# A feed-forward up projection on one Trainium2 core: high and low activations as one product of 512 columns, added by VectorE

## The reference, cut to what matters

```python
def conv_ffn(h, w_up, conv_w, conv_b, w_down):
    a, b = jnp.split(h @ w_up, 2, axis=-1)          # h: 256 x 1024, w_up: 1024 x 5632
    a = causal_depthwise_conv(a, conv_w, width=3) + conv_b
    return (jax.nn.gelu(a) * b) @ w_down            # w_down: 2816 x 1024
```

## Time and profile before

| | |
|---|---|
| Median of 3 runs | 938.27 us (937.1 to 939.4) |
| Profiled execution, its own time | 937.77 us |
| Its span, first to last instruction | 935.9 us |
| Mean granted TensorE clock over the span | 0.979 of full speed |
| Up projection, first product to last | 262.03 to 388.72 us |
| Down projection, first product | 389.73 us |
| The copies of `w_small` and `cmp_w2` | issued at 4.03 and 4.53 us, landed 10.8 and 10.6 us later |
| ScalarE's first use of `w_small` | 15.73 us |

### The profile page before, as it was taken

The page is one execution under the profiler, slowest core; times in us unless marked ns, Lnnn a source line. Parts: engine busy times, 40 slices in busy tenths (PEclk is TensorE's granted clock), DMA queues, the critical chain, the costliest instruction groups (busy, mean ns, idle before and its releaser), DMA issues.

```text
span 935.9 us, 15607 instructions
## 1 busy us (share of the span) xinstructions
PE 884.7 (95%) x6286; PEld 798.9 (85%) x6286; DVE 529.2 (57%) x931; ACT 485.3 (52%) x817; POOL 33.7 (4%) x39
## 2 busy tenths in 40 slices
PE   6999999998999999999899999999899799988987
PEld 6999898888999999987799999888777799975665
DVE  5334356758556666757745333577646736465334
ACT  6643557753465444555643344566655654443334
POOL 0000000007000000000000000000000000000310
PEclk9999999999999999999899999999999899999799
DMA  9655732245525555565354235333337355252031
GB/s 344 252 176 215 275 128 99 91 142 183 173 97 183 182 183 184 174 220 181 98 192 162 91 136 181 135 96 130 106 120 239 129 180 169 102 180 91 0 113 46
DMA packets 21555, 144.54 MB, mean 154 GB/s; under 512 B 2513, under 2 KB 3153, under 8 KB 4720
## 3 DMA queue, kind: packets, MB, share of 16 engines
q1 hardware_dynamic: 20592, 140.55, 43.4%
q10 hardware_dynamic: 896, 3.03, 1.0%
HBM read 142.53 MB, written 1.05 MB: 153 GB/s over the span
## 4 chain that ended last, share of the span: by engine, by line
PE 79%; DVE 9%; ACT 7%; issue 3%; DMA 2%; POOL 0%; DVEq 0%; POOLq 0%; ACTq 0%; SPq 0%
PE PS L417 77%; DVE wl L1582 3%; ACT wh L1088 2%; DMA ring<-w 1%; ACT PB L1122 1%; PE PS L492 1%; ACT L1447 1%; ACT hh L1102 1%; DMA xa<-x 1%; PE PS L1018 0%; ACT L1451 0%; PE PS L688 0%; DVE PB L1985 0%; DVE hl L1602 0%; DVE Y L2009 0%
## 5 line engine op out<-in xcount | busy, mean ns | idle before, releaser
L1582 DVE TENSOR_TENSOR wl<-ring,wh 128x1024 fp32r<-128x1024 f32 x248 | 305.0, 1233 | 312.7 <-ACT wh L1088 305.3
L1088 ACT ACTIVATE wh<-ring 128x1024 fp32r<-128x1024 f32 x248 | 261.2, 1056 | 292.2 <-PE PS L417 273.9
L417 PE MATMUL PS<-hh,wh 128*128 128x256 f32 x1244 | 357.9, 288 | 6.6 <-DVE BIG L2117 3.7
L417 PE MATMUL PS<-hl,wh 128*128 128x256 f32 x1244 | 352.1, 283 | 0.0
L417 PE MATMUL PS<-hh,wl 128*128 128x256 f32 x1244 | 351.9, 283 | 0.0
L417 PEld LDWEIGHTS PS<-hh,wh 128*128 128x128 f32 x1244 | 238.7, 192 | 12.4 <-issue 5.8
L417 PEld LDWEIGHTS PS<-hl,wh 128*128 128x128 f32 x1244 | 238.8, 192 | 0.7 <-issue 0.5
L417 PEld LDWEIGHTS PS<-hh,wl 128*128 128x128 f32 x1244 | 238.7, 192 | 0.0
L417 PE MATMUL PS<-wh,hh 128*128 128x256 f32 (+2 forms) x528 | 177.5, 336 | 10.9 <-DVE hl L1602 5.7
L417 PE MATMUL PS<-wl,hh 128*128 128x256 f32 (+2 forms) x528 | 173.5, 329 | 0.0
L417 PE MATMUL PS<-wh,hl 128*128 128x256 f32 (+2 forms) x528 | 173.4, 328 | 0.0
(11 more groups left out here) (265 smaller groups left out, 719.9 us busy)
## 6 DMA issues: line engine op xcount, KB each, us to landing
ring<-w SPq DMA_DIRECT2D x128, 1024.0 KB, 4.9
cn<-consts SPq DMA_DIRECT2D x2, 1051.0 KB, 9.9
V<-gains ACTq DMA_DIRECT2D x3, 512.0 KB, 4.6
cn<-consts SPq DMA_DIRECT2D x1, 1050.5 KB, 7.4
xa<-x SPq DMA_DIRECT2D x2, 512.0 KB, 4.5
out<-xb SPq DMA_DIRECT2D x4, 256.0 KB, 2.1
cn<-late ACTq DMA_DIRECT2D x1, 704.0 KB, 6.0
cn<-conv ACTq DMA_DIRECT2D x1, 470.0 KB
```

The costliest lines, as they stand in the source:

```text
L417: return nc.tensor.matmul(o, lhsT, rhs, start=start, stop=stop, skip_group_check=True)
L1088: A(wh[:, q % SPLITS, :], ring[:, i % RING, e:e + HALF], ACT.Copy).then_inc(sem("hi_ready"), 1)
L1582: TTn(wl[:, q % SPLITS, :], ring[:, PLACE[unit_of(q)] % RING, e:e + HALF], wh[:, q % SPLITS, :].bitcast(F32), ALU.subtract).then_inc(sem(" ...
```

## The change

Only the 22 up units change. The high and low activations now lie side by side in one tile `hx`, so that the high weights are loaded once and meet high and low activations in one product of 512 columns. A second product of 256 columns adds the low weights. The halves of `a` and `b` land in separate PSUM banks, columns 0 to 255 for the high activations and 256 to 511 for the low ones. ScalarE copies the low columns of both banks to `T1`, VectorE adds the high columns to them, in place, and the tap, the convolution and the product with `b` read `T1`.

```diff
-        hh, hl = sb("hh", [P, KD, S], F32R), sb("hl", [P, KD, S], F32R)
+        hx = sb("hx", [P, KD, 2, S], F32R)
+        hh, hl = hx[:, :, 0, :], hx[:, :, 1, :]
...
+        UP = (0, 2)
...
-            nc.sync.dma_start(w2s[:, :, :, :], cmp_w2).then_inc(sem("cmp_w2_in"), 16)
+            nc.sync.dma_start(w2s[:, :, :, :], cmp_w2).then_inc(sem("w_small_in"), 16)
...
+            def up_unit(i):
+
+                o = UP[i % 2]
+                if i >= 2:
+                    pe.wait_ge(sem("up_read"), i - 1)
+                for half in range(2):
+                    a, b = half_in(half_of("up") + 2 * i + half)
+                    for j in range(2):
+                        for k in range(4):
+                            c_ = slice(k * 256 + j * P, k * 256 + (j + 1) * P)
+                            kk = 4 * half + k
+                            act_in(kk)
+                            mm(PS[:, o + j, :], a[:, c_], hx[:, kk, :, :], kk == 0, False)
+                            m = mm(PS[:, o + j, 0:S], b[:, c_], hh[:, kk, :], False, kk == KD - 1)
+                    half_out(m)
...
             for i in range(NF):
-                wide_b(FIRST["up"] + i)
+                up_unit(i)
...
-            act.wait_ge(sem("w_small_in"), 16)
+            act.wait_ge(sem("w_small_in"), 32)
...
-                A(CV[:, i % 2, 0:S], bank_of(u)[:, 0:S], ACT.Identity, scale=v("conv_w", 2 * NF + i),
+                if i >= 2:
+                    act.wait_ge(sem("up_done"), i - 1)
+                A(cols2(T1[:, i % 2, :]), PS[:, UP[i % 2]:UP[i % 2] + 2, S:2 * S], ACT.Copy).then_inc(sem("up_low"), 1)
+                act.wait_ge(sem("up_read"), i + 1)
+                A(CV[:, i % 2, 0:S], T1[:, i % 2, 0:S], ACT.Identity, scale=v("conv_w", 2 * NF + i),
                   bias=v("conv_b", i)).then_inc(sem("ffn_tap"), 1)
...
                 keep_up(u)
+                dve.wait_ge(sem("up_low"), i + 1)
+                t1 = cols2(T1[:, i % 2, :])
+                TTn(t1, PS[:, UP[i % 2]:UP[i % 2] + 2, 0:S], t1, ALU.add).then_inc(sem("up_read"), 1)
                 dve.wait_ge(sem("ffn_tap"), i + 1)
-                a, cv = bank_of(u)[:, 0:S], T2[:, i % 2, 0:S]
+                a, cv = T1[:, i % 2, 0:S], T2[:, i % 2, 0:S]
                 own(STT(cv[:, 1:S], a[:, 0:S - 1], v("conv_w", NF + i), cv[:, 1:S], ALU.mult, ALU.add))
...
-                freed(TTn(BIG[:, i, :], T2[:, i % 2, S:2 * S], bank_of(u)[:, S:2 * S], ALU.mult), u)
+                TTn(BIG[:, i, :], T2[:, i % 2, S:2 * S], T1[:, i % 2, S:2 * S], ALU.mult)\
+                    .then_inc(sem("up_done"), 1)
```

More of the change, by code:

```diff
@@ L343, in cmpP @@
             return CM[:, (g * 2 + t) * 96:(g * 2 + t + 1) * 96]
-        WIDE = [u for s, n in STREAM if s not in ("cmp", "w_p", "down", "even_out", "w_uq", "w_uk", "w_uv",
+        WIDE = [u for s, n in STREAM if s not in ("cmp", "w_p", "up", "down", "even_out", "w_uq", "w_uk", "w_uv",
                                                   "w_fd", "odd_out")
@@ L622, in cmp_out @@
                 pe.wait_ge(sem("cmp_gelu"), i + 1)
-                pe.wait_ge(sem("cmp_w2_in"), 16)
+                pe.wait_ge(sem("w_small_in"), 32)
                 for g in range(2):
@@ L785, in _ @@
             pe.wait_ge(sem("taps_kept"), 4)
+            for q in range(2):
+                pe.wait_ge(*read(FIRST["w_o"] + 2 + q))
             for i in range(NF):
-                wide_b(FIRST["up"] + i)
+                up_unit(i)
             deep("down", 0, NF, DEEP)
@@ L916, in _ @@
                 wide_b(FIRST["z_d"] + i)
-            pe.wait_ge(sem("late_in"), 16)
+            pe.wait_ge(sem("late_in"), 32)
             pe.wait_ge(sem("lora_rs"), 1)
@@ L1300, in _ @@
             nc.scalar.dma_start(ropes[5].bitcast(I32), positions.broadcast_to([P, S]))\
-                .then_inc(sem("positions_in"), 16)
+                .then_inc(sem("late_in"), 16)
             nc.scalar.dma_start(gB[:, :], gains[0:1, :].broadcast_to([P, D])).then_inc(sem("gains_in"), 16)
@@ L1328, in _ @@
                 if i == NF - 1:
-                    act.wait_ge(*read(FIRST["up"] + DOWN_EARLY - 2))
-                    act.wait_ge(*read(FIRST["up"] + DOWN_EARLY - 1))
+                    act.wait_ge(sem("up_done"), DOWN_EARLY)
                     for k in range(DOWN_EARLY):
@@ L1341, in _ @@
                 if k == DOWN_EARLY:
-                    for i in range(2):
-                        act.wait_ge(*read(FIRST["up"] + NF - 2 + i))
+                    act.wait_ge(sem("up_done"), NF)
                 deep_high("down", BIG, DOWN, k)
@@ L1861, in _ @@
                 halves(half_of("down") + k + 1)
-            dve.wait_ge(sem("positions_in"), 16)
+            dve.wait_ge(sem("late_in"), 16)
             own(nc.vector.tensor_copy(ropes[4], ropes[5].bitcast(I32)))
```

## The result

The changed kernel takes 940.37 us (median of 14 executions, 938.67 to 942.76), the kernel before 938.16 us in 14 executions beside it (936.78 to 939.99). The ratio is 1.0022, 95% interval 1.0012 to 1.0032: 2.2 us slower, which is within the 0.3% that counts as no difference here. I had forecast 7.7 us slower. Executions more than 1.5% longer than the fastest of the same kernel are left out of all ratios and medians here: two of e5_pad22 and seven of e6_fill. The profiled execution took 942.1 us, span 940.3, mean clock 0.982.

The account below looks back on a forecast made before the run. TensorE bounds the kernel before; with the change the ScalarE and VectorE loop bounds the up units. 938.27 us plus 7.7 (6.13 for the later down projection, 1.6 for the clock) gives 946.0 us; range 939.5 to 948.5, eight times in ten.

Parts of the forecast that it names:

- The loop sets the pace: Up units: loop through ScalarE and VectorE takes 6.00 us a unit, above TensorE's 5.55; chance 0.80 for 5.87 to 6.05.
- TensorE's saving: Up units: the wide product saves 13.3 ns a group, at most 4.7 us a stage, but turns into idle time.
- The links: Steps of the ScalarE and VectorE loop in an up unit: 4.71 us before, plus add 0.71 and tap 0.58.
- the tap from SBUF: ScalarE's tap in each up unit, now reading SBUF: taken as 0.55 us, 0.58 with the hand-over.
- First down product: First product of the down projection starts at 395.86 in place of 389.73, 6.13 us later.
- lo2 of unit 0: Second low split of the first up unit, on VectorE: starts at 269.04 in place of 269.25.
- The clock behind the stage: Start of the down projection: some 3.5 us of TensorE idle time lowers its clock, costing 1.6 us.
- The fourth half's split: Down projection: low part ends 7.83 us behind the stage's start, TensorE asks at 8.16; fits by 0.3 us.
- Nothing later gives it back: Stages behind the first down product: the 6.13 us lost there stays lost to the end.
- the third rival: No measurable difference: up loop between 5.62 and 5.83 us through shrinking hand-overs, time 936 to 941 us; chance 0.10.
- the second rival: TensorE keeps the pace in the up units, loop under 5.55 us, time 934.6 us; chance 0.07.

Follow-up runs that it names:

- e5_pad22: Kernel before with 22 one-column memsets added on VectorE in the down projection's loop, nothing else changed: 935.07 us, ratio 0.9966.
- e6_fill: Changed kernel with 14 unread products, 512 columns each as run, ahead of the down projection: 938.35 us, ratio 1.0030, from five of twelve executions.
- e2: Changed kernel with three products of 256 columns per group again in place of the pair: 940.63 us, ratio 1.0028.
- e1: Changed kernel with ScalarE's low copy ahead of the second high split and VectorE's add between the two low splits: 930.46 us, ratio 0.9915.
- e8: Kernel before with three unread products of 256 columns ahead of the third head's scores in the late attention stage: 932.2 us, ratio 0.9937.
- e7: Changed kernel with 234 one-column memsets on VectorE, making 256 instructions more than the kernel before: 945.95 us, ratio 1.0084.
- e9: The reordered kernel of e1 with 234 one-column memsets added on VectorE: 934.2 us, ratio 0.9951.
- e10: Changed kernel with three unread products of 256 columns in the late attention stage, the same as in e8: 940.0 us, ratio 1.0024.
- e3: Kernel before with 39 unread products of 512 columns on TensorE between the up and the down projection: 944.06 us, ratio 1.0062.
- e11_order_gap: The reordered kernel of e1 with the three unread products of e8 in the late attention stage: 928.48 us, ratio 0.9917.

## Why the prediction was right up to 463 us, and wrong behind it

- *The loop sets the pace*: right. 6.07 us a unit where I had 6.00, and TensorE's saving worth nothing (e2). Undoing the order alone takes the loss away (e1: 135.4 us to 125.9 us in the stage).
- *The links*: add to tap 0.72 us (I had 0.71), tap to convolution 0.64 (I had 0.58), the rest as read before. The one mis-sized term is the tap from SBUF: 0.602 us on the mean of 21, where I took 0.55. The upper bound from the nearest rows was 0.58, and was too low as well; the 0.59 worked out from the Trainium skill's page "VectorE: DVE Perf Modes" was nearest.
- *First down product*: predicted +6.13 us, measured +7.88. 20 × 0.07 = 1.4 of the difference is the loop; 0.29 lies ahead of the loop (lo2 of unit 0 starts at 269.33, where I had 269.04; the stage itself began 0.15 later), and 0.06 behind it.
- *The clock behind the stage*: predicted +1.6, measured 1.54, with 3.45 us of idle time for 3.5 and 3.4 us at half clock; e6 shows cause and size.
- *The fourth half's split*: the down projection is longer by the clock's 1.54 us and nothing else (65.86 against 64.32), so it fitted.
- *"Nothing later gives it back"*: this is the step that failed. I looked for something that could absorb a delay and found nothing, rightly for the engines' work. But I took the clock of all later stages as unchanged, put what it could give back at nothing, and didn't read the places where it was low. Of the 9.42 us lost by the end of the down projection 5.08 came back behind it. The late stage of the kernel before lost some 5.6 us (48.5 us against 42.9) to a fall of the clock that hung on TensorE's idle time ahead of 861.33 (e8), 0.35 us of which came with VectorE's 0.40 us; and that comes and goes with the count of VectorE's instructions (e5, e7, e9). The 22 adds took it away. e5 gets this gain without the change, e7 takes it away from the change, e8 gets it by closing the idle time, and with the stage held at full clock the change costs 7.8 us by the medians (e10 against e8). My sum had 7.7, but from a loss 1.5 us too small and a return of nothing where the profiles have 2.6, and the two errors work against each other.
- *Right by the wrong rival*: the time fell where the third rival had it, 936 to 941 us, but by none of its mechanism: the loop was not between 5.62 and 5.83 us. That 940.37 us also lies inside my range, 0.9 above its lower end, is luck: of 7.7 us forecast 2.2 showed.
- *Two slips in the working*: the second rival needs the loop 0.45 us shorter, which is two and a half times the room between 0.42 and 0.60 for the tap and not one and a half. And the Trainium skill, page "TensorE: Matmul & The Clock Gate", section "Back-to-back issue gap", gives N/2.4 + 2.5 ns for an isolated product and says that a stream of products differs; the 0.120 and 0.2267 us of the trace are of a stream, so the formula was no measure for them.

What stays open: the 1.2 us and 1.5 us that came back between 463 and 714 us, where the changed kernel's profile lacks 3.4 us at half clock that the one of before has near 681. e3 shows such a return without any change of VectorE's count, and no run tells what decides it. Nor is it settled what sends the late stage to no, 6.8 or 37.5 us at half clock in kernels without the 0.40 us, all with 0.76 us of idle time ahead of the scores (e2, the changed one, e6): closing the gap is enough to keep the clock up, and 0.76 us in place of 1.11 isn't always. That the 0.40 us is a fetch of instructions is inferred: it goes with 22 instructions more, returns with 256, and a transfer of the instruction queue moves along with it.

## What to carry to other kernels

Ahead of moving work to two engines that are a third idle, add up the loop that runs through both in their written order; where it passes the bound engine's time, put the new operation where the partner has something else to do (e1: the same work, 10 us less, 9.5 of them in the stage). A sum over one stage is a forecast for the kernel only if the rest stays as it is: look for later stages at half clock behind short idle times, since an edit far ahead, even 22 empty instructions, can tip them. Where such a stage is found, hold it down in both kernels before comparing, and consider a few idle products in the gap as a change of its own.

## What the hardware showed that I had not expected

- Three unneeded products of 256 columns in a gap of 1.11 us made the kernel 5.9 us faster (e8).
- 22 memsets of one column made it 3.0 us faster by the medians, 3.2 us by the ratio (e5); 234 made the changed one 5.6 us slower (e7).
- The pair of 512 and 256 columns takes 0.3533 us or 0.3467 us. In e1_order the stage was at 0.3533 and in e11_order_gap, whose code differs only far behind, at 0.3467 in all but its first units; the changed kernel has both in one execution. Over 352 pairs it is 2.3 us, where TensorE sets the pace.
- ScalarE's operation with a scale and a bias per partition took 602 ns from SBUF in the changed kernel (the mean of 21), 590 in e1_order, and 549 from PSUM in the kernel before, 41 to 53 ns apart, where Exp in the earlier trace rows has 27.
